# A hybrid decoder trunk on one core: narrow projection chunk first, its third chunk loaded earlier, fewer dummy products and later bias additions ahead of the pooling

## The reference

```python
def rms_norm(x, gain):
    return x * lax.rsqrt(jnp.mean(x * x, axis=-1, keepdims=True) + EPS) * gain
# layer 0
proj = rms_norm(x, mix_norm_even) @ w_in
au, av, q, kc, vc, ks, vs, kw, vw, gl = jnp.split(proj, split_points, axis=-1)
ya = chunked_spatial_gating(au, av, ...)
# q, ks, kw normalised per head; kc, vc compressed over blocks of 32 tokens;
# o = sigmoid(gl)[0] * o_cmp + sigmoid(gl)[1] * o_sel + sigmoid(gl)[2] * o_win
yb = native_sparse_attention(q, kc, vc, ks, vs, kw, vw, gl, ...)
x = x + jnp.concatenate([ya, yb], -1) @ w_out
x = x + hierarchical_moe(rms_norm(x, ffn_norm[0]), ...)
# layer 1: pooled = mean of the last 2, 4, 8 or 16 tokens, less the token itself
x = x + (einsum('bsgc,gce->bsge', pooled, w_pool) + b_pool) * pool_scale
x = x + hierarchical_moe(rms_norm(x, ffn_norm[1]), ...)
```

## Time and profile before

| | |
|---|---|
| median of 3 runs | 889.72 us (888.76 to 890.54) |
| the profiled execution | 889.84 us |
| its span | 888.1 us |
| TensorE busy | 794.2 us, 89% of the span |
| VectorE, ScalarE, GpSimd busy | 254.7, 242.5, 101.0 us |
| moved from and to HBM | 247.44 and 26.21 MB |

### The profile page before, as it was taken

How to read it: one execution, slowest core, us unless ns; L and a number is a source line. 1 busy time by engine, 2 the same in 40 slices (tenths; PEclk the granted TensorE clock), 3 DMA queues, 4 the chain that set the end, 5 groups by cost and what they waited for, 6 DMA issues and landing times.

```text
span 888.1 us, 10330 instructions
## 1 busy us (share of the span) xinstructions
PE 794.2 (89%) x3981; PEld 376.4 (42%) x3981; DVE 254.7 (29%) x577; ACT 242.5 (27%) x584; POOL 101.0 (11%) x166
## 2 busy tenths in 40 slices
PE   6999899999999989999797888898999996797975
PEld 3447444545455643333232323397433332332321
DVE  0000727565453361111011111655411111111106
ACT  3303355553344401212111111364012211111111
POOL 2000000000001600111001001130111111011000
PEclk9999999999999999999898989999999999889998
DMA  8898130300001997999999999996399999999976
GB/s 291 263 322 190 63 94 2 79 17 1 1 1 53 354 380 288 417 420 421 419 421 419 419 409 373 382 421 266 141 394 419 419 420 422 421 419 417 409 305 254
DMA packets 76048, 258.09 MB, mean 291 GB/s; under 512 B 28129, under 2 KB 29665, under 8 KB 56032
## 3 DMA queue, kind: packets, MB, share of 16 engines
q1 hardware_dynamic: 67072, 241.16, 69.5%
q0 software_dynamic: 8928, 16.27, 4.9%
HBM read 247.44 MB, written 26.21 MB: 308 GB/s over the span
## 4 chain that ended last, share of the span: by engine, by line
PE 74%; DVE 8%; DMA 7%; issue 5%; ACT 3%; SPq 2%; DVEq 0%; POOLq 0%; ACTq 0%
PE ps L1890 24%; PE ps L1904 11%; PE ps L1618 10%; PE ps L1768 6%; PE ps L1884 3%; PE ps L1681 3%; DMA rest<-in_w_exp_down_dram 2%; PE ps L1824 2%; PE ps L1693 2%; PE ps L1836 2%; DVE tmp L1084 2%; PE ps L1598 2%; PE ps L2019 2%; DMA norm<-expert_rows 2%; DMA expert_rows<-tmp 2%
## 5 line engine op out<-in xcount | busy, mean ns | idle before, releaser
L1890 PE MATMUL ps<-w_pair,tmp 128*64 128x512 f32 x704 | 169.2, 636 | 32.8 <-issue 20.1
L1890 PEld LDWEIGHTS ps<-w_pair,tmp 128*64 128x64 f32 x704 | 55.7, 145 | 132.3 <-issue 118.2
L1618 PE MATMUL ps<-w_pair,norm 128*128 128x512 f32 (+1 forms) x256 | 101.2, 555 | 3.1 <-ACT norm L807 3.1
L1084 DVE TENSOR_TENSOR tmp<-tmp,ps 128x256 f32<-128x256 f32 (+1 forms) x34 | 13.8, 407 | 291.8 <-ACT tmp L969 291.7
L1890 PE MATMUL ps<-norm,tmp 128*64 128x512 f32 x320 | 75.6, 626 | 12.9 <-issue 9.2
L969 ACT ACTIVATE tmp<-ps 128x256 f32<-128x256 f32 x32 | 12.3, 385 | 269.3 <-PE ps L1890 269.3
L1904 PE MATMUL ps<-w_pair,tmp 128*64 128x512 f32 x352 | 80.4, 599 | 2.9 <-ACT tmp L972 2.0
L1618 PEld LDWEIGHTS ps<-w_pair,norm 128*128 128x128 f32 x256 | 49.2, 194 | 51.5 <-issue 45.6
L664 POOL DMA_INDIRECT expert_rows<-tmp x30 | 30.1, 1003 | 329.4 <-DVE tmp L1475 329.4
L1768 PE MATMUL ps<-w_pair,norm 128*128 128x512 f32 x128 | 58.0, 593 | 0.0
L964 ACT ACTIVATE tmp<-ps,gains 128x128 f32<-128x128 f32 x128 | 36.6, 368 | 60.7 <-PE ps L1884 60.7
(11 more groups left out here) (247 smaller groups left out, 837.2 us busy)
## 6 DMA issues: line engine op xcount, KB each, us to landing
w_pair<-in_w_exp_gate_dram SPq DMA_DIRECT2D x44, 1024.0 KB
w_pair<-in_w_exp_up_dram SPq DMA_DIRECT2D x44, 1024.0 KB
w_pair<-in_w_exp_down_dram SPq DMA_DIRECT2D x40, 1024.0 KB
rest<-in_w_exp_down_dram SPq DMA_DIRECT2D x20, 1024.0 KB, 23.3
norm<-in_w_exp_gate_dram SPq DMA_DIRECT2D x20, 1024.0 KB, 22.7
norm<-in_w_exp_up_dram SPq DMA_DIRECT2D x20, 1024.0 KB, 29.5
norm<-expert_rows SPq DMA_DIRECT2D x16, 512.0 KB, 8.1
w_pair<-in_w_in_dram SPq DMA_DIRECT2D x3, 2048.0 KB, 11.0
```

Of the source, the lines that this page charges most:

```text
L1084: return ve.tensor_tensor(out, in0, in1, op)
L1618: ins = mm(bank(4 + i % 4)[:, 0:n], xT[:, k, b * P:(b + 1) * P], w[:, k, :], start=(k == 0), stop=(k == KD - 1))
L1890: ins = mm(bank(2)[64 * a:64 * a + 64, :], xgT[:, k, 64 * a:64 * a + 64], gu[w][:, a, :, k * FE:(k + 1) * FE], start=(k == 0), stop=(k == ...
```

## The change

1. *Chunks.* The narrow chunk (280 columns) becomes chunk 0, q chunk 1, kc/vc/ks/vs chunk 2. The first chunk comes in one load.
2. *Loads.* `load_win(2)` and the four compression loads stand ahead of the second half of the first gate/up weights, of the down weights and the zeros.
3. *Dummies at the start.* Four float32 products of the identity with itself, 128 columns wide, between `x_transpose(0)` and `project(0, 0)`.
4. *Statistics.* `mean` is gone from VectorE: ScalarE's root takes the sum of squares with a scale of 1/1024 and a bias column `eps`, which GpSimd sets at the start. The negated `rstd` is gone too; the gates are copied out and all four blocks go through one Exp. ScalarE's wait for all small loads (`s_small`) ahead of the evacuations is gone.
5. *Heads.* ScalarE squares the window key after chunk 0 and q after chunk 1, takes roots of both during chunk 2, and only the selected key (`kv[:, :, 256:384]`) is left for the end of chunk 2. VectorE scales q and the window key during chunk 2, makes the compression inputs, and scales the selected key last.
6. *TensorE's order behind chunk 2.* One q transpose, two k/v transposes, one a_v tile, two q transposes, compression, a_v tile, one q and two k transposes, the last two a_v tiles. Before: two k/v transposes, two a_v tiles, three q transposes, compression, a_v tile, transposes, a_v tile.
7. *Pooling.* GpSimd's bias additions wait until all four blocks are added (`s_cb` 4). The reciprocal of block b − 1 moves between the two additions of `far_rows(0, b)` for b = 2 and 3, and ahead of `last_rows` for b = 1. `keep_warm(18)` becomes `keep_warm(2)`.

```diff
-        CH = [("q", 1024, 512), ("kc_vc_ks_vs", 1536, 512), ("kw_vw_gates", 2048, 280),
+        CH = [("kw_vw_gates", 2048, 280), ("q", 1024, 512), ("kc_vc_ks_vs", 1536, 512),
...
-            w_first = t["w_in"][0].rearrange("(p k) n -> p k n", k=KD)
-            for h in range(2):
-                ks = slice(4 * h, 4 * h + 4)
-                sp.dma_start(win[0].rearrange("p (k n) -> p k n", k=KD)[:, ks, :],
-                             w_first[:, ks, CH[0][1]:CH[0][1] + 512]).then_inc(s_w0b if h else s_w[0], 16)
+            load_win(0)
             for b in range(1, NB):
                 load_x(b)
             load_win(1)
...
             load_gate_up(0, 0, 0)
+            sp.wait_ge(s_pj, 4)
+            load_win(2)
+            sp.wait_ge(s_tp, 2 * NB)
+            for w, name in enumerate(("w_cmp_k", "w_cmp_v")):
+                for g in range(2):
+                    sp.dma_start(wcmp[64 * g:64 * g + 64, w], t[name][0].rearrange("l d e -> d l e"))\
+                      .then_inc(s_wcmp, 16)
             load_gate_up(0, 0, 1)
             load_down(0, 0)
             sp.wait_ge(s_z0, 1)
             sp.dma_start(out_dram.rearrange("(r p) d -> p r d", p=P), zeros.unsqueeze(1).to_broadcast([P, 8, D]))\
               .then_inc(s_zst, 16)
-            for ch in range(2, len(CH)):
+            for ch in range(3, len(CH)):
                 sp.wait_ge(s_pj, 4 * (ch - 1))
                 load_win(ch)
-                if ch == 2:
-
-                    sp.wait_ge(s_tp, 2 * NB)
-                    for w, name in enumerate(("w_cmp_k", "w_cmp_v")):
...
+            g.memset(eps, EPS)
...
             experts(0)
+            pool.wait_ge(s_cb, NB)
             for b in range(NB):
                 pool.wait_ge(s_xs[b], 2)
...
             def root(n, b):
-                act.wait_ge(s_ms, stat(n, b))
+                act.wait_ge(s_sq, NB * n + b + 1)
                 c = slice(n * NB + b, n * NB + b + 1)
-                a.activation(std[:, c], std[:, c], ACT.Sqrt).then_inc(s_sd, 1)
+                a.activation(std[:, c], ssq[:, c], ACT.Sqrt, scale=1.0 / D, bias=eps).then_inc(s_sd, 1)
...
-            act.wait_ge(s_small, SMALL)
...
+            for b in range(NB):
+                proj_tile(0, b)
+            act.wait_ge(s_pe_, 4)
+            a.activation(gate[:, :], gate[:, :], ACT.Exp, scale=-1.0)
+            a.activation(sq2[:, 1], kv[:, :, 512:640], ACT.Square).then_inc(s_hs, 1)
+            for b in range(NB):
+                proj_tile(1, b)
+            act.wait_ge(s_pe_, 8)
+            a.activation(squares.rearrange("p (b c) -> p b c", b=NB), q, ACT.Square).then_inc(s_hs, 1)
+            proj_tile(2, 0)
+            act.wait_ge(s_mean, 1)
+            a.activation(hstd[:, 0:32], hsq[:, 0:32], ACT.Sqrt)
+            a.activation(hstd[:, 40:48], hsq[:, 40:48], ACT.Sqrt).then_inc(s_std, 1)
+            for b in range(1, NB):
+                proj_tile(2, b)
             act.wait_ge(s_pe_, 12)
-            a.activation(squares.rearrange("p (b c) -> p b c", b=NB), q, ACT.Square).then_inc(s_hs, 1)
...
             a.activation(sq2[:, 0], kv[:, :, 256:384], ACT.Square).then_inc(s_hs, 1)
...
+            act.wait_ge(s_mean, 2)
+            a.activation(hstd[:, 32:40], hsq[:, 32:40], ACT.Sqrt).then_inc(s_std, 1)
...
-            def mean(n, b):
-                dve.wait_ge(s_sq, NB * n + b + 1)
-                c = slice(n * NB + b, n * NB + b + 1)
-                ve.tensor_scalar(std[:, c], ssq[:, c], 1.0 / D, EPS, ALU.mult, ALU.add).then_inc(s_ms, 1)
...
-            def far_rows(l, b):
+            def far_rows(l, b, early=None):
                 dve.wait_ge(s_yl[b], 32 * (l + 1))
                 link(ve.scalar_tensor_tensor(x3[:, b, :], YL[:, 0, b, :], far_weight[:, b:b + 1], x3[:, b, :],
                                              ALU.mult, ALU.add))
+                if early is not None:
+                    rroot(2, early)
                 link(ve.scalar_tensor_tensor(x3[:, b, :], YL[:, 1, b, :], far_weight[:, 4 + b:5 + b], x3[:, b, :],
                                              ALU.mult, ALU.add))
...
+            dve.wait_ge(s_hs, 3)
+            link(ve.tensor_reduce(hsq[:, 32:40], sq2[:, 0], AX, ALU.add))
+            head_mean(slice(32, 40)).then_inc(s_mean, 1)
+            dve.wait_ge(s_cz, 2)
+            cmp_input(0)
+            cmp_input(1)
+            dve.wait_ge(s_std, 2)
+            link(ve.reciprocal(hrstd[:, 32:40], hstd[:, 32:40]))
+            k_scaled(0)
...
-                far_rows(0, b)
-                mean(2, b - 1)
+            far_rows(0, 1)
+            rroot(2, 0)
+            last_rows(0, 1, 0)
+            last_rows(0, 1, 1)
+            for b in range(2, NB):
+                far_rows(0, b, b - 1)
                 last_rows(0, b, 0)
-                rroot(2, b - 1)
                 last_rows(0, b, 1)
...
             x_transpose(0)
+            for _ in range(4):
+                mm(bank(7)[:, 0:P], ident[:, :], ident[:, :], start=True, stop=True)
             project(0, 0)
...
-            pe_.wait_ge(s_pe_, 8)
+            pe_.wait_ge(s_qk_n, 4)
+            transpose_blocks(bank(3), q, 2 * P)
+            pe_.wait_ge(s_pe_, 12)
             transpose_blocks(bank(0), kv, 0)
             transpose_blocks(bank(1), kv, P)
             project(3, 0)
-            project(3, 1)
-            pe_.wait_ge(s_qk_n, 6)
             pe_.wait_ge(s_mtv, 1)
             transpose_blocks(bank(0), q, 0)
             pe_.wait_ge(s_mtv, 2)
             transpose_blocks(bank(1), q, P)
-            transpose_blocks(bank(3), q, 2 * P)
...
-            project(3, 2)
+            project(3, 1)
             pe_.wait_ge(s_mta, 1)
             transpose_blocks(bank(0), q, 3 * P)
+            pe_.wait_ge(s_qk_n, 6)
             pe_.wait_ge(s_mta, 2)
             transpose_blocks(bank(1), kv, 256)
             pe_.wait_ge(s_mta, 3)
             transpose_blocks(bank(3), kv, 512)
+            project(3, 2)
             project(3, 3)
...
-            keep_warm(18, bank(0))
+            keep_warm(2, bank(0))
```

More of the change, by code:

```diff
@@ L1140, in _ @@
             x_out(0)
-            mean(0, 0)
             for b in range(1, NB):
@@ L1171, in _, with cmp_input @@
                 ins.then_inc(s_qk_n, 1)
-            dve.wait_ge(s_cz, 2)
-            for r in range(2):
-                dve.wait_ge(s_mt, 1 + r)
+            def cmp_input(r):
+                dve.wait_ge(s_mt, 2 + r)
                 link(ve.tensor_copy(rawT[:, r, :], bank(r)))
@@ L1183, in _ @@
                 ins.then_inc(s_ci, 1)
+            dve.wait_ge(s_hs, 1)
+            ve.tensor_reduce(hsq[:, 40:48], sq2[:, 1], AX, ALU.add)
+            dve.wait_ge(s_hs, 2)
+            link(ve.tensor_reduce(hsq[:, 0:32], squares.rearrange("p (a d) -> p a d", d=HD), AX, ALU.add))
+            head_mean(slice(0, 32))
+            head_mean(slice(40, 48)).then_inc(s_mean, 1)
+            link(ve.tensor_scalar(gate[:, :], gate[:, :], 1.0, None, ALU.add))
+            ve.reciprocal(gate[:, :], gate[:, :])
+            dve.wait_ge(s_std, 1)
+            ve.reciprocal(hrstd[:, 0:32], hstd[:, 0:32])
+            link(ve.reciprocal(hrstd[:, 40:48], hstd[:, 40:48]))
+            qv = q.rearrange("p b (h d) -> p b h d", d=HD)
+            hv = hrstd[:, 0:32].rearrange("p (b h) -> p b h", b=NB)
+            for b in range(NB):
+                tt(qv[:, b], qv[:, b], bc(hv[:, b], 2, [P, NH, HD]), ALU.mult).then_inc(s_qk_n, 1)
+            k_scaled(1)
+            dve.wait_ge(s_hs, 3)
[7 more added lines that the diff above has]
+            k_scaled(0)
             def v_sum(b):
@@ L1512, in _ @@
             raw_out(0, 1)
-            mean(1, 2)
             rroot(1, 2)
@@ L1516, in _ @@
             raw_out(0, 2)
-            mean(1, 3)
             raw_out(0, 3)
@@ L1525, in _ @@
             last_rows(0, 0, 1)
-            for b in range(1, NB):
-                far_rows(0, b)
-                mean(2, b - 1)
+            far_rows(0, 1)
[4 more added lines that the diff above has]
+                far_rows(0, b, b - 1)
                 last_rows(0, b, 0)
-                rroot(2, b - 1)
                 last_rows(0, b, 1)
-                if b >= 2:
-                    pooled_out(b - 2)
-            mean(2, 3)
+                pooled_out(b - 2)
             rroot(2, 3)
@@ L1537, in _ @@
             pooled_out(2)
-            mean(3, 0)
             rroot(3, 0)
@@ L1541, in _ @@
             raw_out(1, 0)
-            mean(3, 1)
             pooled_out(3)
@@ L1546, in _ @@
             raw_out(1, 1)
-            mean(3, 2)
             rroot(3, 2)
@@ L1550, in _ @@
             raw_out(1, 2)
-            mean(3, 3)
             raw_out(1, 3)
```

70 lines of the change are left out of this document (21 added, 49 removed).

## The result

| | before | changed |
|---|---|---|
| median of 7 runs, us | 890.54 (888.76 to 893.94) | 884.98 (879.86 to 885.61) |
| ratio, 95% interval | | 0.9913 (0.9887 to 0.9939) |
| profiled execution, us (span) | 889.84 (888.1) | 885.34 (883.6) |

The kernel is faster, by 5.6 us in the medians. The ratio lies nearer to that of the means, 883.5 against 891.0 us, which are 7.5 apart. Forecast were 883.3 us and a range of 880.3 to 886.8. The spread of the changed kernel alone is 5.8 us, wider than any term of the sum.

A forecast was written before the change was run, and what follows sets the result against it. The prediction took TensorE work, 74% of the span, as the bound, so savings count where they close its holes or start its stretches earlier. Sum: 889.84 + 0.35 − 1.4 − 1.8 − 3.7 = 883.3 us; range 880.3 to 886.8.

The forecast's parts named there:

- Start, +0.35: First projection tile: the larger first load delays it by 0.35 us, ends 0 and +0.9.
- Clock at the start, -1.4: First projection tile: four dummy products bring the clock up earlier, saving 1.4 us, nowhere certain between 0 and 2.45.
- the first rival, at 884.7: Start of the kernel: the dummies change nothing of the clock, 884.7 us; chance 0.22.
- New order of chunks, 0: Projection chunks: reordering costs nothing; the last chunk's weights land at 81 to 83.5 us, needed at 85.5.
- Behind the chunks, -1.8: From the chunks' end to the gate rows: two holes behind VectorE, 2.09 us, become 0.3; gain 1.8 us.
- Pooling, -3.7: Layer 0's pooling: second pooling rows start at 573.97 in place of 577.68; gain 3.7 us, ends 4.6 and −1.9.
- Neither half gives it alone: Pooling: the 3.7 us need both changes; second rows at 576.4 with 18 dummies, about 576 with old adds.
- Rival: additions hold up VectorE: Pooling: VectorE's additions into x wait for all four GpSimd adds; 888.8 us, no difference; chance 0.06.
- Rival: the gain is not carried through the experts: Expert stages: the weight stream sets their pace, so the front's gain is lost; 886.1 us; chance 0.07.
- its own sign: Expert stages: the prediction calls itself wrong if they take longer by what the front saved.

The follow-up runs named there:

- e1: Kernel before with 2 dummies ahead of the pooling in place of 18, nothing else; median 895.41 us, ratio 1.0051.
- e2: Kernel before with GpSimd's bias additions waiting for all four added blocks, nothing else; median 889.91 us, ratio 0.9987.
- e3: Kernel before with 2 pooling dummies in place of 18 and GpSimd's bias additions behind all four blocks; median 891.07 us, ratio 0.9992.
- e9: Kernel before with 10 pooling dummies in place of 18 and GpSimd's bias additions behind all four blocks; median 889.68 us, ratio 0.9995.
- e10: Changed kernel without GpSimd's wait for all four added blocks, so its bias additions start as before; 883.47 us, ratio 0.9921.
- e5: Changed kernel once more, unedited, for a second profile; median 885.80 us, ratio 0.9940.
- e6: Changed kernel without the four dummy products at the start; median 884.50 us, ratio 0.9926.
- e12: Changed kernel with six start dummies in place of four and 52 dummies in place of 46 in layer 0's router; 882.52 us, ratio 0.9904.
- e8: Changed kernel with the old load order: gate/up, down and zeros ahead of chunk 2 and the compression weights; median 896.20 us, ratio 1.0051.

## Why the prediction was right

- **Start, +0.35.** Wrong in sign: -0.25 in this pair. The longer first load did not delay the tile; x's first block came 0.26 us earlier as well, and ScalarE's rows ended the wait in both the earlier trace rows. The trace of before is the earliest of its kind: in e1, e2, e3 and e9, with the same front, the first tile waits for its weights and starts at 9.53 to 10.11, and the six traces with the new front and four dummies have 8.76 to 8.97. By the means of these (9.60 and 8.91) the start gains 0.7 us.
- **Clock at the start, -1.4.** Mis-sized: 0.66 in this trace, 0.4 as a mean of six (2.12 lost, against 2.53 in before and e1, e2, e3 and e9). The step that failed was "If the clock rises 4.9 us after the first product", by which four dummies would have saved 1.3 us; "if the hole of about 1.3 us behind them spoils it, none" was nearer, and with it the first rival, at 884.7. The Trainium skill (TensorE: Matmul & The Clock Gate, Part 1) says that the check runs free of the kernel and that the number of slow products differs between runs; the six values of 5.80 to 6.42 us agree, and so does the tile of 9.13 to 10.04 us in the kernels with the old front.
- **New order of chunks, 0.** Right, with its cover: chunk 3's transfers were over by 80, forecast were 81 to 83.5. The estimate took the 17.0 us of the compression loads over; they took 12.0.
- **Behind the chunks, -1.8.** Measured -1.83 (from the chunks' end to the gate rows 37.65 us, before 39.48).
- **Pooling, -3.7.** The size was right, -3.63; the reason was not. "Neither half gives it alone" holds against e1 and e2, but the pair named is the wrong one. "with the old adds, the first of which would then start just ahead of VectorE's block 2 and shut it out, at about 576" is refuted by e10, where the second rows start 10.84 us after VectorE's first addition, as in the changed kernel. That step of the working left the reciprocal behind the blocked operation, where the change moves it ahead. And the working took the 16 dummies for a cost only. In the profile of e3 the old VectorE order with 2 dummies leaves a hole of 1.8 us and loses 3.4 us of clock behind it. So the two that need each other are the fewer dummies and the early reciprocal (with the removed mean). That the fewer dummies need it is shown by e1 and e3; that it needs them is read from e2's timeline, and how much the clock costs without a profile is open, as above.
- **Rival: additions hold up VectorE.** Didn't happen. GpSimd ran 9.31 us of additions, and VectorE's operation that reads PSUM took 1.22 us among them; the scaled additions with both inputs in SBUF were over by then. The Trainium skill (SBUF — State Buffer, Who interferes with whom) lets a vector operation with two SBUF inputs contend with a GpSimd instruction that reads SBUF, and one with a single SBUF input not. Both sides of it are seen: 1.22 us here, and 2.80 in place of 1.28 in e10.
- **Rival: the gain is not carried through the experts.** The mechanism in it is real, since the stream sets the stage's length, and the reason given against it is real too: the stream starts with TensorE's release of the first pair. A gain ahead of the stage is carried in full (e5: 232.8 us, e6: 232.1, before: 232.0). What the profiled pair of executions lost there, 3.2 us, is of the size of what the clock took at the ends of the stages (1.5 us at layer 0's first gate/up, 1.7 at layer 1's last half), which the prediction did not name at all. The loss is more than the 2.73 us that the front had saved, so by its own sign ("if the experts take longer by what the front saved") the prediction would have failed on this pair; e5 and e6 show that this was not the front's doing. Whether the ends of the stages also make the range between 879.9 and 885.6 is not shown: the shortest and the longest of the seven have the same mean granted clock, 0.969.

The forecast of 883.3 is 1.7 below the median of 884.98 and 0.2 below the mean. In part that is luck. Over all traces the start gives 0.7 us and its dummies 0.4, 1.1 together, where the sum had +0.35 and -1.4, 1.05 together: two misses that cancel. And the pooling's 3.7 came by another pair of edits than the one named. What is left cannot be assigned to a term, as two profiled executions of the changed kernel differ by 2.8 us (885.34 and 882.54).

No version is clearly ahead of the changed kernel. e12, with six dummies at the start, has the lowest median of all (882.52) and reaches the gate rows 1.8 us ahead of it, but its ratio, 0.9904, lies within the changed kernel's interval.

## What to carry to other kernels

Before taking keep-warm products out, look at what the next real product waits for: if that does not come earlier too, the work is replaced by a hole, and the clock behind it can cost more than the products did (e1: +4.4 us for 16 products fewer). When an engine's operation is slowed by a neighbour, first ask what is queued behind it that someone waits for; with that one small operation moved ahead, removing the collision added nothing (e10). In a stage that is paced by a weight stream, count TensorE's time only up to its first release of a buffer and after the last landing.

## What the runs showed of the hardware

- Behind a hole of 1.81 us the granted clock fell to 0.50 in the window 580 to 584 (e3); behind one of 0.34 us in the same place it stayed at 1.00 (e9).
- The clock's level at a given place differs between executions of one kernel, with the same code and nearly the same holes ahead of it: the first gate/up took 8.78 us and 7.09 in the two profiles of the changed kernel. The windows show it, first of the changed kernel, then of e5:

```profile
330.00:339.00 9.00, 9.00 (x36) 2.90 (x35) 0.00 (x0) 0.38 (x1) 0.29 (x1) 0.82 0.39 118
```

```profile
330.00:339.00 9.00, 8.53 (x42) 3.49 (x42) 1.11 (x2) 1.11 (x5) 0.62 (x1) 1.00 0.55 174
```

- At the very start the granted clock says 1.00 while the durations are those of the lower level (9.55 us for a tile of 7.10, window 9 to 13). There only the durations can be trusted.
- The hold of the first two compression loads on the SP queue is not a constant of theirs: 17.0 us from 47.8 in the kernel before, 19.4 from 47.2 in e8, 12.0 from 30.2 in the changed kernel.
